# Attention scores as three 64-row products per component in two row tiles, instead of two 128-row products

## The reference, cut to what matters

```python
q = apply_partial_rope(q, cos, sin).astype(jnp.float32) * (d ** -0.5)   # d = 64
k = apply_partial_rope(k, cos, sin).astype(jnp.float32)
q = q.transpose(0, 2, 3, 1, 4)                # batch, head, component c = 0..1, token, d
...
s = jnp.einsum('bhcqd,bhckd->bhcqk', q_blk, k)
mask = kpos[None, :] <= qpos[:, None]
p = jax.nn.softmax(jnp.where(mask, s, -jnp.inf), axis=-1)
a = p[:, :, 0] - lam * p[:, :, 1]
return jnp.einsum('bhqk,bhkv->bhqv', a, v32)
```

## Time and profile before

| | |
|---|---|
| median of 3 runs | 1898.09 us (1896.85 to 1898.28) |
| span of the profiled execution | 1894.0 us |
| share of that median outside the span | 4.1 us |
| PE busy in the profile | 1883.2 us (99%) |
| DVE, ACT, POOL busy | 63%, 50%, 17% |
| granted TensorE clock | 0.999 of full speed |

### The profile page before, as it was taken

One profiled execution on the slowest core, in us unless ns is written; L12 is line 12 of the kernel. 1 busy time (PEld: TensorE's weight loads), 2 busy tenths in 40 slices (PEclk: granted clock), 3 DMA queues, 4 the chain that ended last, 5 costly groups with the idle time before them and its releaser, 6 DMA issues.

```text
span 1894.0 us, 26953 instructions
## 1 busy us (share of the span) xinstructions
PE 1883.2 (99%) x9960; PEld 1618.3 (85%) x9960; DVE 1197.4 (63%) x1560; ACT 948.6 (50%) x1541; POOL 329.7 (17%) x182
## 2 busy tenths in 40 slices
PE   8999999999999999999999999999999999999998
PEld 6989898989898989888888888888888888888887
DVE  7675758586767667644311122677877778688774
ACT  5455655556565555445333233237576575333343
POOL 2202020211111121232124444430000000021002
PEclk9999999999999999999999999999999999999999
DMA  5341515151424242432254334557677687464322
GB/s 214 116 153 67 179 56 194 50 193 51 164 74 161 83 161 89 143 129 67 71 202 144 139 122 164 194 202 255 216 260 267 205 278 248 176 231 154 145 79 89
DMA packets 103282, 292.85 MB, mean 155 GB/s; under 512 B 10888, under 2 KB 28040, under 8 KB 92192
## 3 DMA queue, kind: packets, MB, share of 16 engines
q1 hardware_dynamic: 100896, 283.36, 43.2%
q10 hardware_dynamic: 2304, 8.39, 1.1%
HBM read 204.61 MB, written 87.10 MB: 154 GB/s over the span
## 4 chain that ended last, share of the span: by engine, by line
PE 98%; DVE 1%; DMA 0%; POOL 0%; ACT 0%; DVEq 0%; issue 0%; POOLq 0%
PE gp L758 14%; PE gp L756 14%; PE gp L757 14%; PE scores L1037 6%; PE scores L1041 6%; PE scores L1039 6%; PE gp L776 3%; PE gp L775 3%; PE gp L774 3%; PE gp L1037 2%; PE gp L1041 2%; PE gp L1039 2%; PE scores L880 2%; PE scores L882 2%; PE ob L930 2%; PE ob L931 2%
## 5 line engine op out<-in xcount | busy, mean ns | idle before, releaser
L756 PE MATMUL gp<-r1h,w_hi 128*128 128x512 f32 x880 | 346.6, 394 | 0.0
L758 PE MATMUL gp<-r1h,w_lo 128*128 128x512 f32 x880 | 343.5, 390 | 0.0
L757 PE MATMUL gp<-r1l,w_hi 128*128 128x512 f32 x880 | 342.8, 390 | 0.0
L1037 PE MATMUL scores<-xh,qh 128*128 128x512 f32 x512 | 199.7, 390 | 0.1
L1041 PE MATMUL scores<-xh,ql 128*128 128x512 f32 x512 | 199.2, 389 | 0.0
L1039 PE MATMUL scores<-xl,qh 128*128 128x512 f32 x512 | 199.2, 389 | 0.0
L758 PEld LDWEIGHTS gp<-r1h,w_lo 128*128 128x128 f32 x880 | 165.1, 188 | 35.1
L756 PEld LDWEIGHTS gp<-r1h,w_hi 128*128 128x128 f32 x880 | 165.3, 188 | 32.7
L757 PEld LDWEIGHTS gp<-r1l,w_hi 128*128 128x128 f32 x880 | 165.4, 188 | 32.5
L1266 ACT ACTIVATE pr<-scores,nb 128x256 f32<-128x256 f32 (+7 forms) x128 | 93.8, 739 | 117.1 <-DVE nb L1695 117.1
L2091 POOL TENSOR_TENSOR w_lo<-w_raw,w_hi 128x1024 fp32r<-128x1024 f32 x25 | 60.6, 2424 | 508.6 <-ACT w_hi L1140 486.4
(11 more groups left out here) (351 smaller groups left out, 4308.5 us busy)
## 6 DMA issues: line engine op xcount, KB each, us to landing
xraw<-xo_d SPq DMA_DIRECT2D x54, 1024.0 KB, 5.1
w_raw<-in_in_blocks SPq DMA_DIRECT2D x64, 512.0 KB, 3.7
proj_d<-ev SPq DMA_DIRECT2D x128, 256.0 KB, 2.2
rq<-in_ff_quarters SPq DMA_DIRECT2D x32, 1024.0 KB, 8.2
xo_d<-res SPq DMA_DIRECT2D x78, 256.0 KB, 3.4
xo_d<-ring SPq DMA_DIRECT2D x60, 256.0 KB, 3.5
gt<-proj_d SPq DMA_DIRECT2D x32, 256.0 KB, 3.4
xt<-in_x_halves SPq DMA_DIRECT2D x8, 512.0 KB, 6.3
```

The costliest lines, as they stand in the source:

```text
L756: pe.matmul(gp[half][:], wh[slot][:, k, :], mh[:, k, t], start=(k == 0), stop=False)
L757: pe.matmul(gp[half][:], wh[slot][:, k, :], ml[:, k, t], start=False, stop=False)
L758: mm = pe.matmul(gp[half][:], wl[slot][:, k, :], mh[:, k, t], start=False, stop=(k == KT - 1))
L1037: pe.matmul(bank, qh[s % 3][:, k, cols], xh[s % 3][:, k, :], start=first and k == 0, stop=False, skip_group_check=True)
```

## The change

Per component three products of 64 contraction rows take the place of the two stacked ones: q high · k high, q low · k high, q high · k low (the low·low term is no longer computed). The operands are `qhi`, `qlo`, `khi`, `klo`, each [128, 1024] in the layout of `qraw`/`kraw`: component 0 on partitions 0 to 63 and component 1 on 64 to 127, so nothing is moved to other partitions. A product of component 0 uses array rows 0 to 63 (a tile of 64 by 128 at row 0), one of component 1 rows 64 to 127 (a tile of 64 by 128 at row 64). The two components alternate. The masks stay products of 128 rows and now both stand ahead of the block's products.

```diff
-            qs = sb("qs", [P, 2, S], F32R, sc)
-            ka = sb("ka", [P, 2, S], F32R, sc)
-            kb = sb("kb", [P, 2, S], F32R, sc)
+            qhi = sb("qhi", [P, S], F32R, sc)
+            qlo = sb("qlo", [P, S], F32R, sc)
+            khi = sb("khi", [P, S], F32R, sc)
+            klo = sb("klo", [P, S], F32R, sc)
...
+                        rows = [slice(c * DK, (c + 1) * DK) for c in range(2)]
+                        at_q = slice(i * P, (i + 1) * P)
                         for c in range(2):
-                            for lo, hi in edges:
-                                diag = lo <= m0 < hi
-                                q = qs[:, c, i * P:(i + 1) * P]
-                                if diag:
-
-                                    pe.matmul(sp_[:, c, m0:m0 + 2 * P], identr[:], mask[:, moff:moff + 2 * P],
-                                              start=True, stop=False, skip_group_check=True)
-                                pe.matmul(sp_[:, c, lo:hi], q, ka[:, c, lo:hi], start=not diag, stop=False,
-                                          skip_group_check=True)
-                                mm = pe.matmul(sp_[:, c, lo:hi], q, kb[:, c, lo:hi], start=False, stop=True,
-                                               skip_group_check=True)
-                            mm.then_inc(s_done, 1)
+                            pe.matmul(sp_[:, c, m0:m0 + 2 * P], identr[:], mask[:, moff:moff + 2 * P],
+                                      start=True, stop=False, skip_group_check=True)
+                        for lo, hi in edges:
+                            diag = lo <= m0 < hi
+                            for n, (q, k) in enumerate(((qhi, khi), (qlo, khi), (qhi, klo))):
+                                for c in range(2):
+                                    mm = pe.matmul(sp_[:, c, lo:hi], q[rows[c], at_q], k[rows[c], lo:hi],
+                                                   start=(n == 0 and not diag), stop=(n == 2), skip_group_check=True)
+                                    if n == 2 and hi == width:
+                                        mm.then_inc(s_done, 1)
...
-                        act.activation(to[0:DK, 0, :], x_[0:DK, :], ACT.Copy).then_inc(qk_hi, 1)
-                        act.activation(to[DK:P, 1, :], x_[DK:P, :], ACT.Copy).then_inc(qk_hi, 1)
-                        if c == 0:
-                            act.activation(kb[DK:P, 0, :], x_[0:DK, :], ACT.Copy).then_inc(qk_hi, 1)
-                            act.activation(kb[0:DK, 1, :], x_[DK:P, :], ACT.Copy).then_inc(qk_hi, 1)
-                            if behind_k:
-                                behind_k()
+                        act.activation(to[:], x_[:], ACT.Copy).then_inc(qk_hi, 1)
+                        if c == 0 and behind_k:
+                            behind_k()
...
+                    def low_part(c, x_, hi, lo):
+                        dve.wait_ge(qk_hi, 2 * h + c + 1)
+                        dve.tensor_tensor(lo[:], x_[:], hi[:].bitcast(F32), ALU.subtract).then_inc(qk_lo, 1)
```

More of the change, by code:

```diff
@@ L472, in row_loads @@
             def row_loads(h):
-                sp.wait_ge(qk_lo, 6 * h + 6)
+                sp.wait_ge(qk_lo, 2 * h + 2)
                 if isinstance(h, int) and h == 0:
@@ L862, in scores @@
                         if i == 0:
-                            pe.wait_ge(qk_lo, 6 * h + 6)
+                            pe.wait_ge(qk_lo, 2 * h + 2)
                             wait(pe, nd_out, 3 * h)
@@ L1226, in attend @@
                     evac_units()
-                    for c, (x_, to) in enumerate(((kraw, ka), (qraw, qs))):
+                    for c, (x_, to) in enumerate(((kraw, khi), (qraw, qhi))):
                         act.wait_ge(roped, 2 * h + c + 1)
-                        act.activation(to[0:DK, 0, :], x_[0:DK, :], ACT.Copy).then_inc(qk_hi, 1)
-                        act.activation(to[DK:P, 1, :], x_[DK:P, :], ACT.Copy).then_inc(qk_hi, 1)
-                        if c == 0:
-                            act.activation(kb[DK:P, 0, :], x_[0:DK, :], ACT.Copy).then_inc(qk_hi, 1)
-                            act.activation(kb[0:DK, 1, :], x_[DK:P, :], ACT.Copy).then_inc(qk_hi, 1)
-                            if behind_k:
-                                behind_k()
+                        act.activation(to[:], x_[:], ACT.Copy).then_inc(qk_hi, 1)
+                        if c == 0 and behind_k:
+                            behind_k()
                     act.wait_ge(v_in, 16 * h + 16)
@@ L1660, in attend @@
                         if x_ is qraw:
-                            low_parts(0, kraw, ka)
+                            low_part(0, kraw, khi, klo)
                         dve.tensor_tensor(x_[:], x_[:], turned[:], ALU.add).then_inc(roped, 1)
@@ L1664, in attend @@
                             weight_low(h + 1, 1)
[L1665 to L1668, removed]
+                    low_part(1, qraw, qhi, qlo)
                     dve.wait_ge(v_hi, h + 1)
```

## The result

The changed kernel takes 1904.49 us (median of 5 runs, 1903.69 to 1906.14) against 1896.85 us for the kernel before, timed beside it. The ratio is 1.0039, 95% interval 1.0027 to 1.0052: by the ratio 7.4 us slower, where 8.1 us less were forecast.

What follows compares the result with a forecast made beforehand. PE's stream of matrix instructions was taken as the bound. Pairs -11.9 us and switches +3.8 us gave -8.1 us: 1890.0 us against a median of 1898.1 us, range 1880 to 1934 us, with 1880 to 1894 us given 0.42.

Steps and rivals of the forecast that it cites:

- What bounds the kernel, and the stream prices: PE's matrix stream sets the time; a product costs 0.231, 0.175 or 0.12 us for 512, 384 or 256 columns.
- What a pair costs: Score products: two 64-row products, one per component, overlap on PE; taken as -11.9 us for all scores.
- two cases: Overlapping score pairs with weight loads side by side, -17.8 us, or with the loads in series, -6.0 us.
- the lower end: Score pairs run side by side and cost one product each: 53.2 us in place of 71.0 us, -17.8 us.
- I take 0.03 us for a switch: Each of 128 changes on PE between 128-row products and 64-row tiles costs 0.03 us, 3.8 us in all.
- upper bound of 0.29 us: Most a switch on PE could cost, if PE ran empty and only then loaded weights; 37 us for 128.
- the switch costs real time: Rival on PE's changes of array shape, listed in the prediction as dear switches: 1902 to 1930 us, chance 0.24.
- No overlap: Rival on score pairs: their products run one behind the other, +35.5 us and the switches, 1934 us and up, chance 0.17.
- ACT and DVE at nothing: Copies and subtractions saved, 4.2 us of ACT and 4.9 us of DVE a head, stand beside PE and gain nothing.
- Waits that could appear ... under 1 us in all: PE waiting for exponentials at block 6: margin still covers; if gone, a tenth of a us a head, under 1 us.
- the narrowest margin: Block 6: PE starts its scores 0.43 us after block 5's last exponential; shorter block 5 eats 0.05 to 0.35 us.
- The 4.1 us around the span: Time outside the profiled span, added to the forecast span of 1885.9 us to give 1890.0 us.

Runs made afterwards that it cites:

- e1: Kernel before, with the second product of each component in a block's last region done twice in its 64-row tile: 1922.42 us, ratio 1.0131.
- e3: Changed kernel with the two masks directly ahead of the diagonal region, 64 switches more, same products: 1917.34 us, ratio 1.0106 to the kernel before.
- e5: Changed kernel with 128-row products, as many as before the change, and masks back in their places: 1896.47 us, ratio 0.9997 to the kernel before.
- e2: Changed kernel with one 128-row product in place of each pair, so no switches: 1888.95 us, ratio 0.9954 to the kernel before.
- e4: Changed kernel with the three products of component 0 in a region ahead of those of component 1: 1905.81 us, ratio 1.0043 to the kernel before.
- e8: Changed kernel with all products of component 0 in a block, both regions, ahead of component 1: 1923.45 us, ratio 1.0137 to the kernel before.
- e7: Changed kernel with row tiles only in blocks 0 to 3, 128-row products in blocks 4 to 7: 1905.41 us, ratio 1.0042 to the kernel before.
- e6: Changed kernel with row tiles only in blocks 4 to 7, 128-row products in blocks 0 to 3: 1898.06 us, ratio 1.0004 to the kernel before.

## Why the prediction was wrong

The forecast sum was -11.9 + 3.8 = -8.1 us; the trace has -17.8 + 25.0 = +7.2 us, and the runs +7.4 us by the ratio.

- **What bounds the kernel, and the stream prices**: right. PE is the bound after too, and 0.231, 0.175 and 0.12 us a product, with the measured switch, carry the sum to within 0.4 us.
- **What a pair costs**: the mechanism was right, the size off. I took the middle of two cases, -11.9 us; the loads of a pair run side by side and the lower end holds, -17.8 us. The Trainium skill's rule of concurrent row tiles ("TensorE: Matmul & The Clock Gate", Part 3) agrees with the trace: the starts of a pair are 0.00 to 0.01 us apart in the rows above.
- **"I take 0.03 us for a switch"**: this step failed, and with it the sign. The switch costs 0.195 us in the trace, 0.196 us in e1, 0.20 us in e3; 128 of them are 25.0 us where 3.8 us stood in the sum. The upper bound of 0.29 us held. The row that I leaned on the earlier trace rows, from float32 to float32r, stays in one array shape. It does cost nothing, as I read it, but I missed why. Two loads of the kernel before show it:

```profile
366.04 0.46 PEld L944 LDWEIGHTS tr<-ident,at 128*128 128x128 f32 x4
366.46 0.19 PEld L756 LDWEIGHTS gp<-r1h,w_hi 128*128 128x128 f32 x1
366.57 0.19 PEld L757 LDWEIGHTS gp<-r1l,w_hi 128*128 128x128 f32 x1
```

The first load of the new kind (366.46) follows the loads of the transposes with no gap of its own, and the next one comes 0.11 us later. The second product of the new kind comes 0.32 us behind the first in place of 0.23 us: this is the uncovered load, the half of the switch price that the trace before did show, and there it was already in the 0.11 us of each transpose. At a change of array shape the load follows products of 256 to 512 columns, which hide a load otherwise, so its 0.10 us come on top, and 0.09 us more. The sentence in the rival, that a load is hidden only because the array takes the next weights behind a product of the same shape, described what happens. The Trainium skill ("TensorEngine Tiling (Array Packing)", Tiling Modes, Key Properties) says that a change of the tiling mode drains the engine; the trace agrees in that the first load behind the change begins 0.09 us late. With no row for the change of shape, I should have put the value between the bounds. At 0.15 us the forecast would have been +7 us; that it comes so close to the result would have been luck, as two errors cancel in it, 0.15 for 0.195 us and -11.9 for -17.8 us.
- **The rival "the switch costs real time"** is the case that came, at 0.20 us; its -11.9 made it +13.7 us in place of +7.4 us. Of the two errors in the forecast, the switches were 21.2 us too cheap and the pairs 5.9 us too dear, so that the second hid part of the first. Block 7, forecast at 1.69 us, took 1.91 us (368.29 to 370.20) and 0.11 us in the distance behind it.
- **No overlap** is ruled out. **ACT and DVE at nothing** is right, shown by e5; the profile has 34.4 us less of ACT and 40.3 us less of DVE, 4.3 and 5.0 us a head where 4.2 and 4.9 us were forecast.
- **"Waits that could appear ... under 1 us in all"**: wrong, though the changed kernel doesn't show it, because the hitches give each block its length back. e2 shows it: an ideal saving of 17.8 us would have been cut to 8.4 us. The waits at the `ob` products behind the scores were not in my list, and the 0.43 us at block 6 that I called the narrowest margin is not the narrowest. In the trace of the kernel before, the subtraction that the `ob` product behind block 7 needs ends at 364.94 + 0.42 = 365.36, and that product starts at 365.66, 0.30 us later:

```profile
364.94 0.42 DVE L1675 TENSOR_TENSOR atl<-tr,ath 128x256 fp32r<-128x256 f32 x1 [0.34 <-ACT ath L1243]
```

- **The 4.1 us around the span** were wrong as well. A run of 1905.43 us has a span of 1903.2 us, 2.2 us around it. The profiled span of 1894.0 us came from an execution without the 2 us at the start, which by the same 2.2 us took an estimated 1896.2 us, not the median of 1898.09 us.

None of the versions run here that do the tiled products beats the kernel before. A block gains one product length per region, 0.12 us (blocks 0, 1) to 0.46 us (block 7), and pays 2 x 0.195 = 0.39 us. Only blocks 6 and 7 come out ahead, by 0.02 and 0.07 us, under 1 us over eight heads, less than a measurement here can tell; that split was not run.

## What to carry to other kernels

Count changes of array shape as you count products: in this kernel each costs 0.2 us, nearly a product of 512 columns, and a session of tiles (from the switch in to the switch out) must save more than two of them. Once in a shape, stay: put all full-array work (here the masks) on one side of the tiled work. And when a stream is shortened, check the margin of every wait behind the shortened place, not of one alone; in e2 a wait cost its own time and then 0.10 us for the weight load that it left uncovered.

## What the runs showed of the hardware that was not expected

- Two row tiles take products from the queue past each other: with three products of the other tile in front (e4) the partner starts 0.01 us behind; with six (e8) its load starts only when three are left in front of it.
- Two 64-row weight loads for different row tiles run side by side: pairs of 256 columns follow every 0.12 us, while single full loads need 0.11 us each.
- The granted clock at the start is not the same in every execution. The runs of before beside e5 lie at 1896.2 to 1896.9 us or at 1897.5 to 1898.5 us, and the mean granted clock is 0.997 or 0.998 in nearly all the longer ones, 0.999 or 1.000 in the shorter. The two traces at hand differ in the same way ahead of the first mask. In the trace of 1903.2 us (rows below) the granted clock is 0.50, the 1.2 GHz level, from 11.6 to 18.4 us, though PE is busy throughout; in the trace of 1894.0 us it is 1.00 there. The 14 products (line 783 before, 784 after) that PE runs in the first 19 us have a median duration of 1.06 us in the trace of 1903.2 us and 0.59 us in the other. The traces of e1, e2, e4, e5 and e7 have such a stretch too, from 11.5 to 12.2 us on, and their first mask at 118.6 us; those of e3, e6 and e8 have none, and their first mask stands at 116.9 to 117.0 us. All of them run the same products ahead of it. Why the clock falls in one execution and not in another stays open.

```profile
L784 PE MATMUL scores<-yrow,ones x14: 592/1061/1220, 2.6 to 18.9; 128*128 128x512 f32 x14
...
11.60:18.40 6.80, 6.80 (x21) 4.74 (x21) 1.55 (x3) 1.29 (x6) 2.74 (x3) 0.50 1.00 367
```

In the last row the first numbers are the stretch and PE's busy time in it, and 0.50 is the granted clock.
